# The first layer's q, k and V projections from high and low parts, in token halves, beside the search of the 256 best keys

## The chip, the cores and the metric

The kernel runs on one core of one Trainium2 chip. The metric is the device time of one execution in microseconds (us), the median of several executions. A core has five engines that run their own instruction queues and meet through semaphores: TensorE (PE; its weight loads are listed as PEld), VectorE (DVE), ScalarE (ACT), GpSimd (POOL) and SyncE (SP), which here only issues DMAs.

## The reference

Two transformer layers in sequence on 1024 tokens of width 1024, all in f32. The change lies in the first layer's start:

```
h = x @ w_in                         # [1024, 3112]; parts of its columns:
a_u, a_v      -> gelu, layer norm of v, gMLP mixer (product with w_s)
b_q, b_k, b_v -> diff_attention: 4 heads, two q/k maps of 64 each, V of 128; bias -slope * |distance|
c_q, c_k, c_v -> dsa_attention over 256 selected keys per query
i_q, i_k, i_w -> score = sum over 8 heads of w * relu(q_i . k_i); the 256 best keys of each query are selected
mix = concat(out_a, out_b, out_c);  x = layer_norm(alpha * x + mix @ w_out);  then a gated FFN
```

The second layer has a forgetting attention, a pool mixer, a short convolution, gates and a second FFN; nothing is changed there but the names of some semaphores.

## The kernel before

The program is one hand-written order of work for each engine. `ORDER` lists the stages; a `Ledger` walks through it and gives each weight chunk a slot of the `ring` (4 slots of 128x1024 f32, filled by SyncE's DMAs; a slot is loaded again once its last user has signalled `weights_used`), each chunk that is split into a high and a low part one of three buffers `w_parts` (`w_high`, `w_low`), and each result a pair of PSUM banks.

Two kinds of product are used. A plain f32 product takes `ring` and f32 tiles directly; the trace lists two records for each. A split product works on `float32r` operands: GpSimd (`split_weight`) writes the high part with a TENSOR_SCALAR and the low part, weight minus high part, with a TENSOR_TENSOR, and TensorE sums three products, high with high, high with low, low with high. All later large stages are split; before the change the first layer's input projections are plain.

The order in the stretch that matters, with the stage names of the code:

- `turn_x`, `idx`, `cv`: x is transposed into `xT` (8 tiles of 128 x 1024 tokens), the index and the sparse V projections are made.
- `score`, mixed with `cqk`: 48 score units on TensorE, ScalarE's relu, VectorE's weighted sum.
- VectorE then searches the 256 best keys: 32 bits of a threshold, from the top one down, for six blocks of queries in two groups. For each bit and group: a TENSOR_SCALAR (L2269) and a SCALAR_TENSOR_TENSOR (L2275) on 128x3 numbers set the next trial threshold, then `count` (L2256) compares three blocks of scores with it and counts, one instruction a block. Each waits for the one before it. Then for each block the ties are ranked and the mask is made (`topk_done`), then comes the layer norm of the gMLP's v (`v_normed`).
- TensorE meanwhile runs the rest of `cqk`, `auv` (gMLP's u and v, by tokens), `turn_ws`, `bqk` (q and k of the differential attention: two times four chunks, `by_feature`) and `bv` (its V, `by_token`), all plain f32, from `xT`.
- It then waits for `v_normed`, makes the gMLP product (L1477), waits until VectorE has taken it out of PSUM, and starts the differential attention (`diff.pe`), whose logits VectorE takes with the bias table `bias8`.
- GpSimd makes `dist` at the start, issues the loads of the small constants, and then waits for the masks (`topk_done`). VectorE makes `bias8` from `dist` before its first other work.

What follows (sparse attention, `out1`, FFN, second layer) is not touched.

Of the kernel before, what the change touches and what calls it, by code (L numbers as in the profile page):

```python
# [13 lines left out]
P = 128  # L14
# [49 lines left out]

def sevens(n):
    return [(1, "seven")] * n
# [14 lines left out]
def down_steps(n_k):  # L81
# [11 lines left out]
    "bqk": (whole(4), [0, 1, 2, 3]),  # L93
    "bv": (whole(4), [None, None, None, 3]),
# [28 lines left out]
         ("bqk", 0), ("bqk", 1), ("bv", 0), ("gmlp", 0), ("ada", 0), ("turn_mix", 0), ("out1", 0), ("turn_mod", 0), ("out1", 1)]  # L123
# [21 lines left out]
class Ledger:  # L145


    def __init__(self):
# [6 lines left out]
        for stage, i in ORDER:  # L155
            chunks, units = STAGES[stage] if stage != "idx" else IDX[i]
            self.pairs_at[stage, i] = list(pairs)
            for c, (dmas, kind) in enumerate(chunks):
                s, q = n_loads % RING, n_halves // 2 % PARTS
# [16 lines left out]
                if kind:  # L176
# [5 lines left out]
                    n_halves += 2  # L182
# [51 lines left out]
def program(nc, t, out):  # L234
    L = Ledger()
    with ExitStack() as ctx:
# [32 lines left out]
        xT = view(0, KT, S)  # L269
# [21 lines left out]
        ranks = view(165.5, S)  # L291
# [7 lines left out]
        dist = view(165.5, S)  # L299
# [126 lines left out]
        dist_made = sem("dist_made")  # L426
        bias_made = sem("bias_made")
        lam_sums = sem("lam_sums")
        lam_exps = sem("lam_exps")
# [4 lines left out]
        norm_var = sem("norm_var")  # L434
        norm_sqrt = sem("norm_sqrt")
# [27 lines left out]
        fl_exp, fl_ln, cum_done = sem("fl_exp"), sem("fl_ln"), sem("cum_done")  # L463
        selw_made, counts_made = sem("selw_made"), sem("counts_made")
        cum_high, cum_split, causal_row_made = sem("cum_high"), sem("cum_split"), sem("causal_row_made")
        pool_w_loaded, pool_w_zeroed = sem("pool_w_loaded"), sem("pool_w_zeroed")
# [664 lines left out]
        def b_bias(u, m):  # L1131
            h, b = heads4[u]
            return bias8[:, h, P * (NB - 1 - b):S], bias_made, 4
# [40 lines left out]
        def after_c(act, u):  # L1174
            rows_c(act, u)
            if u == 4:
                act.wait_ge(norm_var, 2)
                act.activation(o_ssq[:, :], o_ssq[:, :], ACT.Sqrt).then_inc(norm_sqrt, 1)
# [117 lines left out]
        def by_feature(pe, stage, i, source):  # L1296

            for c in range(len(STAGES[stage][0])):
                s, p = L.slot(stage, i, c), L.pair(stage, i, c)
                w = ring[:, s, :].rearrange("p (k n) -> p k n", k=KT)  # L1300
                weights_here(pe, stage, i, c)
                pair_here(pe, stage, i, c)
                for h in HALVES:
                    for k in range(KT):
                        mm = pe.matmul(PS[:, 2 * p + h, :], w[:, k, :], source[:, k, half_of(h)],  # L1305
                                       start=(k == 0), stop=(k == KT - 1))
                mm.then_inc(weights_used[s], 1)

        def by_token(pe, stage, source, width=512):

            for c in range(4):
                s = L.slot(stage, 0, c)
                weights_here(pe, stage, 0, c)
                for k in (2 * c, 2 * c + 1):
                    for b in range(NB):
                        p = L.pair(stage, 0, b // 2)
                        if k == 0 and b % 2 == 0:
                            pair_here(pe, stage, 0, b // 2)
                        mm = pe.matmul(PS[:, 2 * p + b % 2, 0:width], source[:, k, tok(b)],  # L1319
                                       ring[:, s, (k % 2) * width:(k % 2 + 1) * width],  # L1320
                                       start=(k == 0), stop=(k == KT - 1))
                        if k == KT - 1 and b % 2 == 1 and b < NB - 1:
                            mm.then_inc(psum_full[p], 1)
                mm.then_inc(weights_used[s], 1)
# [65 lines left out]
        def _(pe):  # L1390
# [68 lines left out]
            by_token(pe, "auv", xT)  # L1459
# [191 lines left out]
        def _(act):  # L1651
# [89 lines left out]
            act.wait_ge(lam_sums, 2)  # L1741
# [25 lines left out]
            for c in range(2):  # L1767
                copy_cqk(1, c)
# [1381 lines left out]
```

## Time and profile before

| | |
|---|---|
| median of 3 runs | 2914.8 us (2908.94 to 2917.13) |
| profiled execution | 2907.3 us, span of its instructions 2905.6 us |
| busy: PE, DVE, ACT, POOL | 2804.6, 1528.2, 932.2, 1278.1 us |
| mean granted TensorE clock | 0.994 |

A busy time is the sum over an engine's instructions. The span is that from the first to the last instruction of the program.

### The profile page before, as it was taken

The numbers are of one execution on the slowest core, as the hardware profiler recorded it, in microseconds if no ns is written. First come the engines' busy times: TensorE is split into PE (matmuls) and PEld (weight loads), VectorE is DVE, ScalarE is ACT, GpSimd is POOL, SyncE is SP. The second block draws the span as 40 slices with busy tenths as digits, with TensorE's granted clock in tenths as the row PEclk, the third lists the DMA queues.
The fourth block names the chain that finished last, engine by engine and source line by source line (L and its number), as shares of the span: only waits on it lengthen the run. The fifth ranks groups of instructions, "written<-read, shape, count | busy, mean of one in ns | idle before, by whom it ended". The sixth has DMA issues, their size and how long they took to land.

```text
span 2905.6 us, 33901 instructions
## 1 busy us (share of the span) xinstructions
PE 2804.6 (97%) x12861; PEld 2071.6 (71%) x12861; DVE 1528.2 (53%) x2414; ACT 932.2 (32%) x1590; POOL 1278.1 (44%) x848
## 2 busy tenths in 40 slices
PE   8999999889999999999999999988999899999998
PEld 5444457468888888887778888855466788888886
DVE  0599977656723334243652203556536722235998
ACT  2401036541233332112333200156103344444443
POOL 2000000036777776666677677700126587753020
PEclk9999999999999999999999999999999999999999
DMA  5111137233422223534433333200556333346854
GB/s 114 30 36 37 40 93 195 88 119 119 131 84 87 87 87 116 211 141 168 129 105 116 123 95 97 71 1 1 180 158 197 117 116 108 117 166 220 280 191 172
DMA packets 343393, 344.59 MB, mean 119 GB/s; under 512 B 18368, under 2 KB 261312, under 8 KB 343232
## 3 DMA queue, kind: packets, MB, share of 16 engines
q1 hardware_dynamic: 319424, 275.33, 30.7%
q10 hardware_dynamic: 21328, 59.97, 5.3%
q0 software_dynamic: 2480, 7.13, 1.0%
q8 instruction: 103, 1.69, 0.2%
q14 instruction: 58, 0.48, 0.0%
HBM read 284.61 MB, written 57.77 MB: 118 GB/s over the span
## 4 chain that ended last, share of the span: by engine, by line
PE 86%; DVE 7%; ACT 2%; issue 2%; DMA 1%; ACTq 0%; POOL 0%; SPq 0%; DVEq 0%; POOLq 0%
PE PS L535 25%; PE PS L1355 13%; PE PS L1367 11%; PE PS L851 9%; PE PS L1319 5%; PE PS L1305 4%; PE PS L1598 4%; PE PS L965 3%; PE PS L1436 2%; PE PS L983 2%; PE PS L1003 2%; PE PS L1547 1%; PE PS L1409 1%; PE PS L995 1%; PE PS L1450 1%
## 5 line engine op out<-in xcount | busy, mean ns | idle before, releaser
L2844 POOL TENSOR_SCALAR w_parts<-ring 128x1024 fp32r<-128x1024 f32 x166 | 205.5, 1238 | 802.3 <-DMA ring<-in_w_out 276.7
L594 DVE TENSOR_TENSOR arena<-arena,PS 128x512 f32<-128x512 f32 x266 | 182.9, 687 | 538.6 <-PE PS L535 537.3
L2847 POOL TENSOR_TENSOR w_parts<-ring,w_parts 128x1024 fp32r<-128x1024 f32 x166 | 445.3, 2682 | 13.8
L851 PE MATMUL PS<-w_parts,hid_high 128*128 128x512 f32 x896 | 276.4, 390 | 5.7 <-DVE w_parts L816 4.1
L535 PE MATMUL PS<-tx_high,w_parts 128*128 128x512 f32 x832 | 264.5, 389 | 0.0
L1355 PE MATMUL PS<-hT_high,w_parts 128*128 128x512 f32 x800 | 248.7, 391 | 7.9 <-DVE hT_low L2439 6.5
L1367 PE MATMUL PS<-w_parts,hid_high 128*128 128x512 f32 x704 | 218.3, 391 | 3.9 <-DVE hid_low L636 2.2
L573 POOL TENSOR_TENSOR w_parts<-arena,w_parts 128x512 fp32r<-128x512 f32 x152 | 194.4, 1291 | 44.6 <-ACT w_parts L554 44.5
L573 POOL TENSOR_TENSOR w_parts<-ring,w_parts 128x512 fp32r<-128x512 f32 x114 | 147.3, 1292 | 131.5 <-ACT w_parts L554 131.5
L851 PEld LDWEIGHTS PS<-w_parts,hid_high 128*128 128x128 f32 x896 | 167.7, 188 | 42.6 <-DVE w_parts L816 6.3
L1355 PEld LDWEIGHTS PS<-hT_high,w_parts 128*128 128x128 f32 x800 | 150.4, 188 | 41.1 <-DVE hT_low L2439 8.2
L535 PEld LDWEIGHTS PS<-tx_high,w_parts 128*128 128x128 f32 x832 | 156.2, 188 | 32.3
L851 PE MATMUL PS<-w_parts,hid_low 128*128 128x512 f32 x448 | 174.3, 389 | 0.0
L1073 DVE CUSTOM_DVE_ANT_0 arena<-PS,arena 128x1024 f32<-128x1024 f32 (+7 forms) x160 | 114.8, 755 | 110.7 <-PE PS L971 53.1
L2256 DVE TENSOR_SCALAR_CACHE_REDUCE arena<-arena,misc 128x384 bf16<-128x384 f32 (+2 forms) x192 | 171.4, 942 | 2.2
L535 PE MATMUL PS<-tx_low,w_parts 128*128 128x512 f32 x416 | 161.8, 389 | 0.0
L1355 PE MATMUL PS<-hT_low,w_parts 128*128 128x512 f32 x400 | 155.8, 389 | 0.0
L1367 PEld LDWEIGHTS PS<-w_parts,hid_high 128*128 128x128 f32 x704 | 132.7, 189 | 32.1 <-issue 4.7
L2907 POOL CAST arena<-ident 128x128 bf16<-128x128 f32 x1 | 0.3, 290 | 335.8 <-DVE arena L2298 335.8
L554 ACT CAST w_parts<-arena 128x512 fp32r<-128x512 f32 x152 | 93.7, 618 | 143.0 <-PE PS L535 120.7
L1319 PE MATMUL PS<-ring,arena 128*128 128x512 f32 (+1 forms) x384 | 138.8, 523 | 0.0
L535 PE MATMUL PS<-x1T_high,w_parts 128*128 128x512 f32 x432 | 138.8, 389 | 0.0
(358 smaller groups left out, 5827.6 us busy)
## 6 DMA issues: line engine op xcount, KB each, us to landing
ring<-in_w_in SPq DMA_DIRECT2D x96, 512.0 KB, 3.7
arena<-hid_spill SPq DMA_DIRECT2D x172, 256.0 KB, 3.7
hid_spill<-arena ACTq DMA_DIRECT2D x54, 512.0 KB, 2.9
ring<-in_w_gu SPq DMA_DIRECT2D x52, 512.0 KB, 3.9
ring<-in_w_ada SPq DMA_DIRECT2D x48, 512.0 KB, 5.3
ring<-in_w_ff SPq DMA_DIRECT2D x96, 256.0 KB, 2.9
ring<-in_w_down SPq DMA_DIRECT2D x44, 512.0 KB, 3.7
ring<-in_w_ff SPq DMA_DIRECT2D x40, 512.0 KB, 4.1
```

Source lines behind the costliest of these rows:

```text
L535: mm = pe.matmul(self.product(g, m), w[:, at], x[:, k, :], start=(k == 0 and i == 0), stop=(k == 3 and i == 2))
L573: pool.tensor_tensor(low, self.raw(n), high.bitcast(F32), ALU.subtract).then_inc(self.split_low, 1)
L594: dve.tensor_tensor(out, a, self.product(g, m), ALU.add).then_inc(self.combined, 1)
L851: mm = pe.matmul(PS[:, 4 * (p % 2) + u, :], x, w, start=(j == 0 and i == 0), stop=(j == self.n_k - 1 and i == 2))
L1305: mm = pe.matmul(PS[:, 2 * p + h, :], w[:, k, :], source[:, k, half_of(h)], start=(k == 0), stop=(k == KT - 1))
L1319: mm = pe.matmul(PS[:, 2 * p + b % 2, 0:width], source[:, k, tok(b)], ring[:, s, (k % 2) * width:(k % 2 + 1) * width], start=(k == 0), sto ...
L1355: mm = pe.matmul(PS[:, 2 * p + bank, :], w[:, q, k * P:(k + 1) * P], x[:, k, half_of(h)], start=(k == order[0] and n == 0), stop=(k == ord ...
L1367: mm = pe.matmul(PS[:, 2 * p + half, :], x[:, k, at], w[:, q, half_of(half)], start=(first and n == 0), stop=(last and n == 2))
L1598: mm = pe.matmul(PS[:, 2 * p + 1, :], w[:, k, :], x[:, half_of(h)], start=(k == ks[0]), stop=(k == ks[-1]))
L2256: stepped(dve.tensor_scalar(tested[b], score[b], threshold(column[b]), None, op, ALU.add, accum_out=enough[:, column[b]:column[b] + 1]))
L2844: pool.tensor_scalar(w_high[:, q, :], ring[:, s, :], 1.0, 1.0, ALU.mult, ALU.mult).then_inc(weights_high, 1)
L2847: pool.tensor_tensor(w_low[:, q, :], ring[:, s, :], w_high[:, q, :].bitcast(F32), ALU.subtract).then_inc(weights_used[s], 1)
```

## The change

- `bqk` and `bv` become split stages. They are done by halves of the tokens: q and k for tokens 0 to 511 (eight chunks), V for them (four chunks), then the same for tokens 512 to 1023. Each weight chunk is so loaded and split twice: 24 loads and splits in place of 12 loads.
- Kind "two" of a chunk: it uses only buffers 1 and 2 of `w_parts` in turn, since buffer 0 shares its memory with live data.
- x itself is needed in a high and a low part. ScalarE copies the high part of a half into free memory (`high_in`), GpSimd subtracts it from `xT` and writes the low part in place (`low_in`), eight tiles of 128x512 for each half. For the second half, the high part overwrites the first half's low part, tile by tile, once the V product of that tile has been made.
- `auv` does its last chunk tile by tile, so that its first tokens' results are complete earlier.
- The bias table moves: `dist` is made by GpSimd after `topk_done`, with the absolute value built from two halves, ScalarE scales it into `bias8`, GpSimd sets the masked corner.
- ScalarE's work is put into one list, `beside_bit`; VectorE's search is as before. Semaphores are merged (`lam_step`, `norm_step`, `fl_step`).

```diff
-    "bqk": (whole(4), [0, 1, 2, 3]),
-    "bv": (whole(4), [None, None, None, 3]),
+    "bqk": (alternate(8), [1, 3, 5, 7]),
+    "bv": (alternate(4), [None, 3]),
...
-         ("bqk", 0), ("bqk", 1), ("bv", 0), ("gmlp", 0), ("ada", 0), ("turn_mix", 0), ("out1", 0), ("turn_mod", 0), ("out1", 1)]
+         ("bqk", 0), ("bv", 0), ("bqk", 1), ("bv", 1), ("gmlp", 0), ("ada", 0), ("turn_mix", 0), ("out1", 0), ("turn_mod", 0), ("out1", 1)]
...
-                s, q = n_loads % RING, n_halves // 2 % PARTS
+                s, q = n_loads % RING, 1 + n_parts % 2 if kind == "two" else n_halves // 2 % PARTS
...
+        def xin(h):
+            return (bqkT_r, xT_r)[h], xT_r
+
+        def in_features(pe, h):
+            x_high, x_low = xin(h)
+            for c in range(8):
+                p, q = L.pair("bqk", h, c // 2), L.part("bqk", h, c)
+                split_here(pe, "bqk", h, c)
+                if c % 2 == 0:
+                    pair_here(pe, "bqk", h, c // 2)
+                for k in range(KT):
+                    if c == 0:
+                        pe.wait_ge(xin_low, KT * h + k + 1)
+                    at = slice(k * P, (k + 1) * P)
+                    pe.matmul(PS[:, 2 * p + c % 2, :], w_high[:, q, at], x_high[:, k, half_of(1 - h)],
+                              start=(k == 0), stop=False)
+                    pe.matmul(PS[:, 2 * p + c % 2, :], w_high[:, q, at], x_low[:, k, half_of(h)], start=False, stop=False)
+                    mm = pe.matmul(PS[:, 2 * p + c % 2, :], w_low[:, q, at], x_high[:, k, half_of(1 - h)],
+                                   start=False, stop=(k == KT - 1))
+                mm.then_inc(parts_used[q], 1)
...
-            by_token(pe, "auv", xT)
+            by_token(pe, "auv", xT, by_tile=True)
...
-            by_feature(pe, "bqk", 0, xT)
-            by_feature(pe, "bqk", 1, xT)
-            by_token(pe, "bv", xT)
+            for h in HALVES:
+                in_features(pe, h)
+                in_tokens(pe, h)
...
+            def high_in(h, k):
+                for b in range(4 * h, 4 * h + 4) if k == 0 else ():
+                    freed(act, "turn_x", b // 4, b % 4)
+                if h == 1 and k % 2 == 0:
+                    q = L.part("bv", 0, k // 2)
+                    act.wait_ge(parts_used[q], L.part_uses("bv", 0, k // 2) + 1)
+                act.copy(xin(h)[0][:, k, half_of(1 - h)], xT[:, k, half_of(h)]).then_inc(xin_high, 1)
...
-            act.wait_ge(bias_made, 4)
+            act.wait_ge(dist_made, 5)
+            for h in range(4):
+                act.activation(bias8[:, h, :], dist, ACT.Copy, scale=-8.0 * SLOPES[h]).then_inc(dist_made, 1)
+            act.wait_ge(dist_made, 5 + 4)
...
-            dve.wait_ge(dist_made, 1)
-            do(dve.scalar_tensor_tensor(out=dist, in0=dist, scalar=-1.0, in1=dist, op0=ALU.mult, op1=ALU.max))
-            for h in range(4):
-                do(dve.tensor_scalar(bias8[:, h, :], dist, -8.0 * SLOPES[h], None, ALU.mult))
-                dve.memset(bias8[0:64, h, S - 64:S], NEG).then_inc(bias_made, 1)
...
+            def low_in(h, k):
+                pool.wait_ge(xin_high, KT * h + k + 1)
+                pool.tensor_tensor(xT_r[:, k, half_of(h)], xT[:, k, half_of(h)],
+                                   xin(h)[0][:, k, half_of(1 - h)].bitcast(F32), ALU.subtract).then_inc(xin_low, 1)
+
+            for c in range(2):
+                split_weight("bqk", 0, c)
+            for k in range(KT):
+                if k % 2 == 0 and k < 6:
+                    s = L.slot("auv", 0, k // 2)
+                    pool.wait_ge(weights_used[s], L.slot_uses("auv", 0, k // 2) + 1)
+                if k == 6:
+                    unit_here(pool, "auv", 0, 1)
+                low_in(0, k)
+            for c in range(2, 8):
+                split_weight("bqk", 0, c)
+            for c in range(3):
+                split_weight("bv", 0, c)
+            low_in(1, 0)
+            low_in(1, 1)
+            split_weight("bv", 0, 3)
+            low_in(1, 2)
+            low_in(1, 3)
+            split_weight("bqk", 1, 0)
+            low_in(1, 4)
+            low_in(1, 5)
+            split_weight("bqk", 1, 1)
+            low_in(1, 6)
+            low_in(1, 7)
+            for c in range(2, 8):
+                split_weight("bqk", 1, c)
+            for c in range(4):
+                split_weight("bv", 1, c)
             pool.wait_ge(topk_done, NB - 2)
+            pool.iota(dist, pattern=[[-1, S]], base=S - P, channel_multiplier=1,
+                      allow_small_or_imprecise_dtypes=True).then_inc(dist_made, 1)
...
```

`in_tokens` makes the V products in the same way: for each chunk two k tiles, four token tiles, three products. SyncE's list of loads follows the new order of stages.

## Rows read from the trace of the kernel before

**Rows 1.** The page's first part: TensorE's busy time, share, instructions.

```profile
PE 2804.6 (97%) x12861; PEld 2071.6 (71%) x12861; DVE 1528.2 (53%) x2414; ACT 932.2 (32%) x1590; POOL 1278.1 (44%) x848
```

**Rows 2.** Chain of waits, 180 to 410 us: start, duration, what.

```profile
181.81 54.93 PE PS L1319 x128
...
237.18 109.87 PE PS L1305 x256
347.05 54.93 PE PS L1319 x128
401.98 3.43 PE PS L1477 x8
```

**Rows 3.** Timeline of VectorE: start, duration, line, operation, idle time before it.

```profile
155.67 0.17 DVE L2269 TENSOR_SCALAR misc<-misc 128x3 int32<-128x3 f32 x1
...
347.80 0.17 DVE L2281 TENSOR_SCALAR misc<-misc 128x6 f32<-128x6 f32 x1
...
391.05 2.29 DVE L2318 TENSOR_TENSOR arena<-arena 128x2048 f32<-128x2048 f32 x1
403.74 1.54 DVE L2325 SCALAR_TENSOR_TENSOR arena<-PS,misc,arena 128x512 f32<-128x512 f32 x2 [10.40 <-PE PS L1477]
```

**Rows 4.** Chain of waits, second layer's V stage.

```profile
1848.29 43.53 PE PS L1547 x192
```

**Rows 5.** The page's DMA issues: count, KB each, us to landing.

```profile
ring<-in_w_in SPq DMA_DIRECT2D x96, 512.0 KB, 3.7
```

**Rows 6.** GpSimd's instructions that write w_parts: ns min/median/max.

```profile
L2844 POOL TENSOR_SCALAR w_parts<-ring x166: 1041/1049/3098, 617.7 to 2339.2; 128x1024 fp32r<-128x1024 f32 x166
L2847 POOL TENSOR_TENSOR w_parts<-ring,w_parts x166: 2352/2394/4376, 618.8 to 2340.3; 128x1024 fp32r<-128x1024 f32 x166
...
L573 POOL TENSOR_TENSOR w_parts<-ring,w_parts x114: 1285/1291/1313, 807.4 to 2568.7; 128x512 fp32r<-128x512 f32 x114
```

**Rows 7.** VectorE's search by groups (busy us, mean ns), one masking instruction.

```profile
L2256 DVE TENSOR_SCALAR_CACHE_REDUCE arena<-arena,misc 128x1024 bf16<-128x1024 f32 x32 | 40.8, 1274 | 0.0
...
L2269 DVE TENSOR_SCALAR misc<-misc 128x3 int32<-128x3 f32 x64 | 10.5, 163 | 0.0
L2275 DVE SCALAR_TENSOR_TENSOR misc<-misc 128x3 int32<-128x3 int32 x62 | 10.1, 163 | 2.1
...
369.67 0.75 DVE L2286 TENSOR_SCALAR arena<-arena,misc 128x1024 bf16<-128x1024 f32 x1
```

**Rows 8.** Timelines of VectorE and GpSimd around 1838 us.

```profile
1838.23 0.91 DVE L2666 TENSOR_TENSOR arena<-arena 64x16 f32<-64x16 f32 x1
1839.17 0.17 DVE L2667 TENSOR_TENSOR arena<-arena 64x16 f32<-64x16 f32 x1
1839.38 3.29 DVE L2668 SCALAR_TENSOR_TENSOR arena<-arena 64x1008 f32<-64x1008 f32 x1
...
1837.60 1.52 POOL L2844 TENSOR_SCALAR w_parts<-ring 128x1024 fp32r<-128x1024 f32 x1 [0.86 <-PE PS L1355]
1839.20 2.40 POOL L2847 TENSOR_TENSOR w_parts<-ring,w_parts 128x1024 fp32r<-128x1024 f32 x1
```

**Rows 9.** The same around 678 us, and one line's durations.

```profile
678.20 1.43 DVE L2378 BATCH_NORM_STATS2 misc<-arena 128x6 f32<-128x512 f32 x2
...
677.60 2.39 POOL L2847 TENSOR_TENSOR w_parts<-ring,w_parts 128x1024 fp32r<-128x1024 f32 x1
...
L2381 DVE TENSOR_SCALAR misc<-misc x4: 170/521/1649, 681.6 to 1418.9; 128x4 f32<-128x4 f32 x4
```

**Rows 10.** TensorE's timeline at 130 us, and a 2 us stretch's sums.

```profile
130.76 3.52 PE L1436 MATMUL PS<-arena,ring 128*128 128x512 f32 x4 [2.99 <-ACT arena L1755]
...
132.00:134.00 2.00, 2.00 (x3) 0.42 (x2) 0.00 (x0) 0.00 (x0) 0.00 (x0) 0.52 0.00 0
```

In the second row the columns are the stretch, its length, the busy us (and instructions) of PE, PEld, DVE, ACT and POOL, the granted TensorE clock, the DMA share and GB/s.

**Rows 11.** Costliest groups of ScalarE: busy us, mean ns.

```profile
L1033 ACT ACTIVATE arena<-arena,misc 128x1024 f32<-128x1024 f32 x20 | 22.9, 1151 | 13.1 <-DVE misc L1073 13.1
```

More of the change, by code:

```diff
@@ L1294, in rows_out, with by_token @@
             act.dma_start(ada_dram[:, 512 * g:512 * (g + 1)], ada_row[0:P:32, g % 2, :]).then_inc(ada_stored, 16)
[L1296 to L1309, printed above, removed]
+        def by_token(pe, stage, source, width=512, by_tile=False):
             for c in range(4):
@@ L1313, in by_token @@
                 weights_here(pe, stage, 0, c)
-                for k in (2 * c, 2 * c + 1):
[L1315 to L1322, printed above, removed]
+                steps = ([(k, b) for b in range(NB) for k in (2 * c, 2 * c + 1)] if by_tile and c == 3 else
+                         [(k, b) for k in (2 * c, 2 * c + 1) for b in range(NB)])
@@ new lines, in by_token @@
+                for k, b in steps:
+                    p = L.pair(stage, 0, b // 2)
+                    if k == 0 and b % 2 == 0:
+                        pair_here(pe, stage, 0, b // 2)
+                    mm = pe.matmul(PS[:, 2 * p + b % 2, 0:width], source[:, k, tok(b)],
+                                   ring[:, s, (k % 2) * width:(k % 2 + 1) * width],
+                                   start=(k == 0), stop=(k == KT - 1))
+                    if k == KT - 1 and b % 2 == 1 and b < NB - 1:
+                        mm.then_inc(psum_full[p], 1)
@@ new lines, in in_tokens @@
+        def in_tokens(pe, h):
+            x_high, x_low = xin(h)
+            for c in range(4):
+                q = L.part("bv", h, c)
+                split_here(pe, "bv", h, c)
+                for k in (2 * c, 2 * c + 1):
+                    at = slice((k % 2) * 512, (k % 2 + 1) * 512)
+                    for n in range(4):
+                        p = L.pair("bv", h, n // 2)
+                        if k == 0 and n % 2 == 0:
+                            pair_here(pe, "bv", h, n // 2)
+                        high, low = x_high[:, k, tok(4 * (1 - h) + n)], x_low[:, k, tok(4 * h + n)]
+                        pe.matmul(PS[:, 2 * p + n % 2, :], high, w_high[:, q, at], start=(k == 0), stop=False)
+                        pe.matmul(PS[:, 2 * p + n % 2, :], high, w_low[:, q, at], start=False, stop=False)
+                        mm = pe.matmul(PS[:, 2 * p + n % 2, :], low, w_high[:, q, at], start=False, stop=(k == KT - 1))
+                        if k == KT - 1 and n == 1:
@@ new lines, in _ @@
+            pool.iota(behind, pattern=[[1, P]], base=0, channel_multiplier=-1,
+                      allow_small_or_imprecise_dtypes=True).then_inc(dist_made, 1)
+            pool.wait_ge(dist_made, 2)
+            for part in (dist[:, S - P:S], behind):
+                pool.tensor_scalar(part, part, 0.0, None, ALU.max).then_inc(dist_made, 1)
+            pool.wait_ge(dist_made, 4)
+            pool.tensor_tensor(dist[:, S - P:S], dist[:, S - P:S], behind, ALU.add).then_inc(dist_made, 1)
+            for h in range(4):
+                pool.wait_ge(dist_made, 5 + h + 1)
+                pool.memset(bias8[0:64, h, S - 64:S], NEG).then_inc(bias_made, 1)
```

129 lines of the change are left out of this document (77 added, 52 removed).

## The prediction

> **What bounds the kernel now.** I read the page first: TensorE is busy for 97% of the span [rows 1], so the reader should expect most of any TensorE saving to arrive, unless another engine stands right behind it. Then the chain of waits through the edited stretch [rows 2]: the gMLP projection (`auv`) runs from 181.81 to 236.74, the q/k products (`bqk`) take 109.87 us, the V products (`bv`) 54.93 us, and at 401.98 the gMLP product (L1477) starts. TensorE never waits in there. Then VectorE's timeline beside it [rows 3]: the search of the 256 best keys runs without a break from 155.67 to 347.80, 64 steps (32 bits, two groups of blocks) of 3.00 us each; ranks, masks and the gMLP normalisation end at 391.05 + 2.29 = 393.34; VectorE then idles 10.40 us until the gMLP product. L1477 waits for both engines. So TensorE sets the time here, but VectorE is only 401.98 - 393.34 = 8.6 us behind. That is the first thing to see: no saving on TensorE can give more than 8.6 us, whatever its size.
>
> **TensorE's part.** Removed: 192 plain f32 products of 128x512, 164.8 us (two records each, 0.858 us a product). Added: 24 chunks (8 q/k and 4 V chunks for each token half) of 24 high/low products, 576 in all. The V stage of the second layer has the same instruction, 192 in 43.53 us, 0.2267 us each [rows 4]: 5.44 us a chunk, 130.6 us in all. The first chunk can start on time. The ring slots come free as `auv` chunks end, the first at 181.81 + 13.73 = 195.5, and a weight load lands in 3.7 us [rows 5], so at 199.2 GpSimd can split; a split is 1.05 us for the high part and 2.39 us for the low part, a low part of x (128x512) 1.29 us [rows 6]. Two splits and eight low parts are 17.2 us, and the last of them waits for the fourth `auv` chunk's first eight products, until about 229, before TensorE is free at 237.18.
>
> In steady state a chunk costs GpSimd 3.52 us with its gap against 5.44 us on TensorE: no stall. At the change of halves, counted from the end of the first V chunk, GpSimd has low parts between the splits: two splits, each followed by two low parts (12.3), the split of the second half's first q/k chunk (15.8), two low parts (18.5), the next split (22.0), two low parts (24.7). TensorE reaches that q/k chunk at 16.3 and should leave it at 21.8, but its last k tile comes at 24.7, and it leaves at 25.4: a stall of 3.6 us. So TensorE ends at 237.18 + 130.6 + 3.6 = 371.4, 30.6 us sooner. That is hidden: it is 22 us ahead of VectorE's 393.34.
>
> **VectorE's part.** Its own work in the stretch is unchanged. Taken off it is the bias table, which lay in idle time at the start and gives nothing. What is new is GpSimd's company: it did nothing during the search, and now has 24 splits and 16 low parts, 24 x 3.44 + 16 x 1.29 = 103.2 us of work, between 199.2 and the last split. That one starts when the chunk two before the last is off TensorE, 371.4 - 10.9 = 360.5, and ends at 364. All of this lies beside the search.
>
> A search step is a TENSOR_SCALAR and a SCALAR_TENSOR_TENSOR on 128x3 (163 ns each), then three counts at about 1.2 ns an element (128x1024: 1274 ns) [rows 7]. What do such operations do beside GpSimd? A 64x16 TENSOR_TENSOR with two SBUF inputs that starts at 1838.23 takes 0.91 us and ends 0.02 us after GpSimd's instruction (1837.60 + 1.52); the next, before GpSimd's next one, takes 0.17; the one at 1839.38 takes 3.29 us because GpSimd holds on until 1841.60 [rows 8]. A 128x4 TENSOR_SCALAR takes 170 ns or 1649 ns. The large single-input BATCH_NORM_STATS2 runs its usual 0.7 us each in the middle of GpSimd's 2.39 us [rows 9]. So the two small operations of each step should wait for GpSimd's current instruction to end, and the counts should not. A TENSOR_SCALAR that writes bf16 without a count takes 0.75 us on 128x1024, the count 1.27 us [rows 7]: the count does not run at the double rate, which is why I put it with the unaffected ones.
>
> The Trainium skill ("GPSIMD Engine Reference", Key points) says that GpSimd shares its SBUF interfaces with VectorE and contends with instructions in a two-port mode or with two SBUF inputs; the trace agrees (0.91 and 3.29 us above), and by that rule the search is no longer undisturbed once GpSimd works beside it.
>
> The price. A step that arrives at random in the 165 us from 199.2 to 364 waits on average (24 x (1.05²/2 + 2.39²/2) + 16 x 1.29²/2) / 165 = 95.1 / 165 = 0.58 us for the first small operation. GpSimd may also start an instruction in the 0.19 us between the two small ones: 0.19 x 103.2 / 165, about 0.12 us, less the cases where the first has just waited. Together 0.69 us. A step then takes 3.69 us, 44.7 of them fit into the 165 us, and they lose 30.9 us. Low end: only the second operation waits, 165 / 3.58 x 0.58 = 26.6 us, and as the two engines are both periodic the phase may take some 6 us off that, 20. High end of this kind: after each wait the other small operation is caught too, and one search step passes per chunk: 24 x (5.44 - 3.00) = 58.6 us. I take 30.9, since in [rows 8] the operation right behind a waiting one slips through in 0.17 us. Highest: the counts wait too, at most all of GpSimd's work, 103 us.
>
> The Trainium skill ("VectorE: DVE Perf Modes", Mode 2×_2P) lets a one-tensor operation use both ports where its outermost dimension is even, or odd and equal on both sides; 128x3 to 128x3 would then be caught. No row here has a 3-wide operation beside GpSimd; without the rule the lost time would be the 26.6 us above and the result +19.9 us.
>
> **The join.** The gMLP product starts when VectorE is through: 393.34 + 0.1 + 30.9 = 424.3. TensorE has then idled from 371.4, 53 us. After a wait of only 2.99 us at 130.76 its granted clock stood at 0.52 (the 1.2 GHz level), and four records took 3.52 us where L1477 needs 1.72 for four [rows 2, 10]: 1.8 us more. From there on everything is as before. ScalarE and GpSimd also build the bias table after the search. GpSimd's few small operations start when the masks are done, 17 us before the join; ScalarE has the square root 9.7 us after the masks, two copies, then four copies of 128x1024 at about 1.15 us [rows 11]: ready about when the normalisation ends, and first needed some 16 us later. Nothing, and with that cover gone 4.6 us.
>
> Sum: -8.6 + 0.1 + 1.8 + 30.9 = **+24.2 us**. The profiled execution took 2907.3 us for its span of 2905.6, 7.5 us under the median of the three shown; the difference put on the median gives 2914.8 + 24.2 = **2939 us**.
>
> **Rivals.**
> 1. *No collision* (not slower). The 3-wide operations pass beside GpSimd, or hold the interface too briefly to wait. For it: no row shows that width; against: every two-input operation of 16 or 8 elements that meets GpSimd's instruction waits. It gives -8.6 + 0.1 + 1.8 = -6.7 us, 2908, inside what can be told from no change. The sign turns measurable at a lost search time of 6.7 + 8.7 = 15.4 us, 0.31 us a step.
> 2. *Both small operations are caught*: 58.6 - 6.7 = up to +52 us, 2967. For it: the gap between high and low split is only 0.08 us, so a race of 0.02 us decides; against: the pair at 1838.23 and 1839.17.
> 3. *The counts are caught too*: up to 103.2 - 6.7 = +96 us, 3011. Against: BATCH_NORM_STATS2. For: the counts read a threshold from SBUF as well.
> 4. *TensorE becomes the bound* because GpSimd starves it: it would have to lose 53 us on top of 3.6, more than half of GpSimd's whole work. Under 1 in 50.
> 5. *A gain that can be measured*: over 0.3% faster needs 8.7 us, and VectorE leaves 8.6 less the cold clock; only scatter gets there.
>
> **Numbers.** 0.3% (8.7 us) is about what a measurement of this kernel can tell from no change. My forecast 0.60, with its own range 2928 to 2946 (lost time 20 to 38 us). Rival 2 0.15, rival 3 0.06, no collision 0.12, a weaker collision near the turning point 0.04, rivals 4 and 5 together 0.03. Range 2925 to 2971: it takes in the forecast and rival 2, and leaves out rival 3 and most of the no-collision case. Slower 0.83 (forecast, 2, 3 and half of the weaker collision), same 0.13, faster 0.04.
>
> **What the profile after would show.** Right: L2269 and L2275 with a mean well above 163 ns, together about 30 us more busy time over their 126 instructions, the counts still 1274 ns, the search ending near 379 and L1477 starting near 424, TensorE idle for about 50 us before it with a granted clock near 0.5 at the restart; w_parts products from 237 to about 371. Wrong: small operations at 163 ns with L1477 near 393 (rival 1), longer counts (rival 3), or L1477 released by TensorE's own work (rival 4). The prediction fails if the race behind a waiting operation goes the other way, or if the 3-wide operations are exempt.

## The result and the profile after

The changed kernel takes 2947.85 us (median of four, 2947.45 to 2950.32) against 2912.83 us (median of four) for the kernel before on the same chip: ratio 1.0122, 95% interval 1.0104 to 1.0139, slower. Forecast were 2939 us and slower. The range 2925 to 2971 holds the result; the narrower range of the main forecast, 2928 to 2946, does not. The profiled execution took 2947.9 us for a span of 2946.2, 40.6 above the span of before; the difference of the medians is 35.0, since the profiled run of before was a short one. The terms below are compared within the spans.

The page of the changed kernel, its first part and the row of the granted clock:

```profile
span 2946.2 us, 34405 instructions
PE 2779.2 (94%) x13046; PEld 2112.4 (72%) x13053; DVE 1568.7 (53%) x2405; ACT 945.2 (32%) x1610; POOL 1391.0 (47%) x920
...
PEclk9999959999999999999999999999999999999999
```

Beside [rows 1]: TensorE has 25 us less work and the kernel is longer, so the engine that fell (97% to 94% of the span) is not what sets the time. VectorE's work rose by 40.5 us though its list of work did not grow (it even lost the bias table): something it does has become slower. The row of the granted clock (PEclk, in tenths of full speed for 40 equal slices) shows a 5 at one place, where TensorE idled. The groups of VectorE's instructions between 150 and 440 us, by shape, say what became slower (instructions | busy us, mean ns | idle before):

```profile
L2333 DVE TENSOR_SCALAR misc<-misc 128x3 int32<-128x3 f32 x64 | 44.5, 695 | 0.0
L2320 DVE TENSOR_SCALAR_CACHE_REDUCE arena<-arena,misc 128x1024 bf16<-128x1024 f32 x32 | 40.8, 1275 | 0.0
...
L2339 DVE SCALAR_TENSOR_TENSOR misc<-misc 128x3 int32<-128x3 int32 x62 | 19.4, 312 | 2.1
```

These answer [rows 7]; L2269, L2275 and L2256 are now L2333, L2339 and L2320. 64 and 62 instructions that took 163 ns each, 10.5 + 10.1 us in all, take 44.5 + 19.4 us, 43.3 us more. The count is where it was, 1275 ns against 1274. A waiting operation shows as a long one here, not as idle time before it (0.0): idle columns would have missed all of it.

VectorE's timeline at the end of the search and at the end of the normalisation, of the changed kernel:

```profile
389.79 1.14 DVE L2320 TENSOR_SCALAR_CACHE_REDUCE arena<-arena,misc 128x896 bf16<-128x896 f32 x1
...
390.97 0.17 DVE L2345 TENSOR_SCALAR misc<-misc 128x6 f32<-128x6 f32 x1
...
434.35 2.29 DVE L2382 TENSOR_TENSOR arena<-arena 128x2048 f32<-128x2048 f32 x1
```

The search ends at 390.97, in [rows 3] at 347.80. The rest of VectorE's stretch, the ranks, masks and normalisation (the rank part, below), has its old length, 45.7 us against 45.5, and it ends at 434.35 + 2.29 = 436.64. The chain of waits there, and the granted clock in windows of 2 us (us, then each engine's busy time, the clock, DMA share, GB/s):

```profile
431.11 5.64 issue
436.75 6.05 PE PS L1509 x8
```

```profile
436.00:438.00 2.00, 1.25 (x2) 0.77 (x3) 0.64 (x1) 0.62 (x1) 0.79 (x1) 0.50 0.00 0
438.00:440.00 2.00, 2.00 (x3) 0.74 (x3) 0.00 (x0) 0.00 (x0) 0.00 (x0) 0.50 0.00 0
440.00:442.00 2.00, 2.00 (x4) 0.86 (x3) 1.43 (x2) 0.00 (x0) 0.00 (x0) 0.62 0.00 0
442.00:444.00 2.00, 0.79 (x2) 0.00 (x0) 1.20 (x3) 0.00 (x0) 0.00 (x0) 1.00 0.00 0
```

TensorE's V products end at 373.43. It idles for 63 us until the gMLP product (L1509, L1477 before), which runs at 0.50, the 1.2 GHz level, for its first 3 us and more, and takes 6.05 us for what took 3.43 in [rows 2]. The first logits of the differential attention on ScalarE, in the changed kernel and in the kernel before:

```profile
447.96 1.15 ACT L1037 ACTIVATE arena<-arena,misc 128x1024 f32<-128x1024 f32 x1 [11.34 <-DVE misc L1077]
```

```profile
410.58 1.15 ACT L1033 ACTIVATE arena<-arena,misc 128x1024 f32<-128x1024 f32 x1 [5.95 <-DVE misc L1073]
```

They start 37.4 us later, which is -8.6 (slack) + 0.1 (handover) + 43.3 + 2.6 (cold clock). The other 3.2 us between the spans are scattered over small waits after that point; I did not trace them to a cause.

How a wait comes about: some of VectorE's small operations (the counts between them are left out) and GpSimd's instructions in one stretch of the changed kernel.

```profile
249.28 0.17 DVE L2333 TENSOR_SCALAR misc<-misc 128x3 int32<-128x3 f32 x1
249.47 2.23 DVE L2339 SCALAR_TENSOR_TENSOR misc<-misc 128x3 int32<-128x3 int32 x1
...
254.15 0.51 DVE L2333 TENSOR_SCALAR misc<-misc 128x3 int32<-128x3 f32 x1
254.69 0.16 DVE L2339 SCALAR_TENSOR_TENSOR misc<-misc 128x3 int32<-128x3 int32 x1
...
260.49 2.08 DVE L2333 TENSOR_SCALAR misc<-misc 128x3 int32<-128x3 f32 x1
...
248.13 1.05 POOL L2909 TENSOR_SCALAR w_parts<-ring 128x1024 fp32r<-128x1024 f32 x1 [1.92 <-PE PS L1335]
249.27 2.42 POOL L2912 TENSOR_TENSOR w_parts<-ring,w_parts 128x1024 fp32r<-128x1024 f32 x1
253.57 1.06 POOL L2909 TENSOR_SCALAR w_parts<-ring 128x1024 fp32r<-128x1024 f32 x1 [1.88 <-PE PS L1335]
254.71 2.42 POOL L2912 TENSOR_TENSOR w_parts<-ring,w_parts 128x1024 fp32r<-128x1024 f32 x1
259.01 1.05 POOL L2909 TENSOR_SCALAR w_parts<-ring 128x1024 fp32r<-128x1024 f32 x1 [1.88 <-PE PS L1335]
260.15 2.40 POOL L2912 TENSOR_TENSOR w_parts<-ring,w_parts 128x1024 fp32r<-128x1024 f32 x1
```

Three cases in eleven microseconds. At 254.15 the TENSOR_SCALAR meets the high split (253.57 + 1.06 = 254.63) and ends at 254.66; the next operation slips into the 0.08 us before the low split. At 260.49 it meets the low split and waits until 262.57, 0.02 us after its end. At 249.28, within 0.01 us of the start of a low split, it just gets through, and the SCALAR_TENSOR_TENSOR behind it waits until that split ends (249.47 + 2.23 = 251.70 against 249.27 + 2.42 = 251.69). The Trainium skill ("SBUF — State Buffer", Who interferes with whom) says that VectorE and GpSimd share a pair of ports under a lock held for a whole instruction, and that a VectorE instruction with one SBUF input outside a two-port mode is free of it; the trace agrees with both, by the ends of the waits and by the counts' 1275 ns.

### The profile page after: what moved, and what is told of

Read it like the earlier page. It is cut to its first block, busy times and chain, and to the rows that moved or that the text cites. A ratio compares the mean times of both kernels' runs of the same rounds, so it can differ in the third digit from the quotient of the medians.

```text
span 2946.2 us, 34405 instructions
## 1 busy us (share of the span) xinstructions
PE 2779.2 (94%) x13046; PEld 2112.4 (72%) x13053; DVE 1568.7 (53%) x2405; ACT 945.2 (32%) x1610; POOL 1391.0 (47%) x920
## 4 chain that ended last, share of the span: by engine, by line
PE 77%; DVE 17%; issue 3%; ACT 2%; DMA 1%; ACTq 0%; POOL 0%; DVEq 0%; SPq 0%; POOLq 0%
PE PS L539 24%; PE PS L1387 13%; PE PS L1399 11%; PE PS L855 9%; DVE arena L2320 6%; PE PS L1630 4%; PE PS L969 3%; PE PS L987 2%; PE PS L1007 2%; PE PS L1579 1%; PE PS L1441 1%; DVE misc L2333 1%; PE PS L999 1%; PE PS L1482 1%; PE PS L1311 1%
## 5 line engine op out<-in xcount | busy, mean ns | idle before, releaser
L2909 POOL TENSOR_SCALAR w_parts<-ring 128x1024 fp32r<-128x1024 f32 x190 | 236.4, 1244 | 996.7 <-DMA ring<-in_w_out 281.3
L2912 POOL TENSOR_TENSOR w_parts<-ring,w_parts 128x1024 fp32r<-128x1024 f32 x190 | 501.0, 2637 | 15.8
L855 PE MATMUL PS<-w_parts,hid_low 128*128 128x512 f32 x448 | 174.3, 389 | 0.0
L2320 DVE TENSOR_SCALAR_CACHE_REDUCE arena<-arena,misc 128x384 bf16<-128x384 f32 (+2 forms) x192 | 171.5, 943 | 2.3
L1399 PE MATMUL PS<-w_parts,hid_low 128*128 128x512 f32 x352 | 137.6, 391 | 0.0
L969 PE MATMUL PS<-arena 64*128 64x512 f32 (+2 forms) x480 | 119.1, 525 | 18.4 <-DVE misc L1077 15.5
```

The costliest lines, as they stand in the source:

```text
L855: mm = pe.matmul(PS[:, 4 * (p % 2) + u, :], x, w, start=(j == 0 and i == 0), stop=(j == self.n_k - 1 and i == 2))
L969: mm = pe.matmul(PS[:, 2 * m + c // 512, 0:w], self.q(j, m, b), self.k(j, m, c, w), start=True, stop=more[m] is None)
L1399: mm = pe.matmul(PS[:, 2 * p + half, :], x[:, k, at], w[:, q, half_of(half)], start=(first and n == 0), stop=(last and n == 2))
L2320: stepped(dve.tensor_scalar(tested[b], score[b], threshold(column[b]), None, op, ALU.add, accum_out=enough[:, column[b]:column[b] + 1]))
L2909: pool.tensor_scalar(w_high[:, q, :], ring[:, s, :], 1.0, 1.0, ALU.mult, ALU.mult).then_inc(weights_high, 1)
L2912: pool.tensor_tensor(w_low[:, q, :], ring[:, s, :], w_high[:, q, :].bitcast(F32), ALU.subtract).then_inc(weights_used[s], 1)
```

## The experiments

Times are medians with their ratio to the kernel before on the same chip (2911.2 to 2911.9 us), where more than one run was made. "Lost" is the busy time of the search's two small operations above their undisturbed time: 10.5 + 10.1 us with two groups [rows 7], 5.5 + 5.1 us with one group (as in e6). Of each edit the main lines are shown.

**e1: GpSimd's work left out.** The high and low parts of this stretch are not made (zeros stand in for both parts of the weights, x's high part for its low part), so q, k and V are not the reference's; everything else of the change stays.

```
+                if stage in ("bqk", "bv"):
+                    pool.sem_inc(weights_high, 1)
+                    pool.sem_inc(weights_used[s], 1)
+                    return
```

> The changed kernel with GpSimd's 24 splits and 16 low parts left out: TensorE runs the same 576 products on the same schedule, but on parts that nobody computed (zeros for the weights, the high part in place of x's low part), so q, k and V are not the reference's. Theory (VectorE's two small operations of each search step wait for GpSimd's instructions): L2333 and L2339 are back at 163 ns, the search takes 192.1 us again, VectorE is through at about 393, and the time is that of before - 8.6 + 0.1 + 2.6 (cold restart of TensorE) = -5.9 us, about 2907. Rival (the loss comes from the doubled weight loads, the cold clock or the new order on ScalarE): still 2935 or more, with the search no shorter than in the changed kernel.

2903.14 us, ratio 0.9969 (0.9958 to 0.9981). The two groups of VectorE's small operations in this kernel:

```profile
L2333 DVE TENSOR_SCALAR misc<-misc 128x3 int32<-128x3 f32 x64 | 10.5, 164 | 0.0
L2339 DVE SCALAR_TENSOR_TENSOR misc<-misc 128x3 int32<-128x3 int32 x62 | 10.1, 162 | 2.1
```

The search ends at 348.66, L1509 starts at 394.44. GpSimd's company costs the whole loss: 44.7 us lie between this kernel and the changed one. Without it the change gains 8.1 us (5.5 to 12.2 by the interval). VectorE's slack less the cold clock is -8.6 + 0.1 + 2.1 = -6.4 us, and the first logits start 5.4 us sooner than in the kernel before; TensorE is done 25.8 us before L1509, and that gains nothing.

**e2: GpSimd's instructions in quarters.** The changed kernel, each split in 128x256 pieces, each low part of x in two.

```
+                for r in at:
+                    ins = pool.tensor_scalar(w_high[:, q, r], ring[:, s, r], 1.0, 1.0, ALU.mult, ALU.mult)
```

> The changed kernel, but each of GpSimd's 128x1024 instructions of the split as four of 128x256, each low part of x as two of 128x256: the same result. Theory (a small operation waits for the end of the one instruction that GpSimd is in): a wait is at most about 0.66 us, the search loses 15 to 22 us in place of 43, time 2922 to 2929. Rival (the loss goes with GpSimd's total busy time, whatever the length of an instruction): 43 us lost as before, about 2948 or a little more.

2925.15 us, 1.0052 (1.0035 to 1.0069), as expected. The same work of GpSimd in smaller instructions loses 17.4 us in place of 43.3.

**e3 and e4: dummy work of GpSimd beside the kernel before.** Subtractions on free memory beside its search, each waiting for the one before: 40 of 128x1024, or 160 of 128x256.

```
+            for r in range(40):
+                do(pool.tensor_tensor(scratch[:, 2, 0:1024], scratch[:, 0, 0:1024], scratch[:, 1, 0:1024], ALU.subtract))
```

> The kernel before, with forty TENSOR_TENSORs of 128x1024 added on GpSimd from the start of the search, on free memory, each waiting for the one before; the products stay plain f32. Theory with lock-step (a released step starts right after an instruction's end, so it meets the second next one's end): a step takes two GpSimd periods of about 2.5 us, 5.0 us in place of 3.0; 20 steps in 100 us, 40 us lost, +34 us after the 8.6 us of slack and 2.6 us of cold clock, about 2947. Random arrival, as in the prediction's sum: 1.2 us a step, 28 us lost, about 2935. No collision: 2913.

> The same with 160 instructions of 128x256, each about 0.66 us with 0.15 us between: the same amount of elements. Theory: a wait is at most 0.66 us; some 15 us lost, +9 us, about 2922. Rival (the loss goes with GpSimd's total busy time): as much as with the forty long ones. No collision: 2913.

2940.55 and 2912.08 us, one run each. The groups of e3, then of e4:

```profile
L2270 DVE TENSOR_SCALAR misc<-misc 128x3 int32<-128x3 f32 x64 | 47.5, 741 | 0.0
L2276 DVE SCALAR_TENSOR_TENSOR misc<-misc 128x3 int32<-128x3 int32 x62 | 10.0, 162 | 2.1
L2911 POOL TENSOR_TENSOR arena<-arena 128x1024 f32<-128x1024 f32 x40 | 94.3, 2358 | 3.1
```

```profile
L2270 DVE TENSOR_SCALAR misc<-misc 128x3 int32<-128x3 f32 x64 | 19.4, 304 | 0.0
L2276 DVE SCALAR_TENSOR_TENSOR misc<-misc 128x3 int32<-128x3 int32 x62 | 10.1, 162 | 2.1
L2911 POOL TENSOR_TENSOR arena<-arena 128x256 f32<-128x256 f32 x160 | 116.6, 729 | 12.5
```

94.3 us of long instructions lose 36.9 us, 116.6 us of short ones 9.0: it is the length of an instruction that VectorE pays for, not GpSimd's busy time. Both sizes were missed: e3's time lies between the two expectations (2947 in lock-step, 2935 for random arrival), so that only the trace decides between them, and e4 lost 9.0 us where 15 were expected. With a semaphore's gap between GpSimd's instructions the second small operation never waits. And the waits are not random ones. Three in a row of the first small operation in e3, where a random arrival would wait 1.2 us on average (an estimate, half of an instruction's 2.36 us):

```profile
232.98 1.84 DVE L2270 TENSOR_SCALAR misc<-misc 128x3 int32<-128x3 f32 x1
...
237.46 2.25 DVE L2270 TENSOR_SCALAR misc<-misc 128x3 int32<-128x3 f32 x1
...
242.75 1.84 DVE L2270 TENSOR_SCALAR misc<-misc 128x3 int32<-128x3 f32 x1
```

A wait puts VectorE at the end of a GpSimd instruction, from where its next steps come at fixed distances. From 232.98 to 242.75 two steps take 9.77 us, which is four instructions of GpSimd's 2.43 us spacing. From 164.77 to 247.22 all eighteen waits alternate between 1.83 to 1.84 and 2.23 to 2.25 us: the two engines lock in phase.

**e5 and e6: one group of blocks.** The search's six blocks in one group, so 32 steps of 128x6, in the changed kernel (e5) and in the kernel before (e6).

```
-            groups = ((2, 3, 7), (4, 5, 6))
+            groups = ((2, 3, 4, 5, 6, 7),)
```

> The changed kernel with the search's six blocks in one group: a bit has one pair of small operations on 128x6 in place of two on 128x3, the same counts, the same result. Theory (the loss is a wait for each pair that meets GpSimd): undisturbed the search would take 32 x 5.7 = 182 us, 10 less; some 26 pairs meet GpSimd at 0.7 to 1.1 us each, 18 to 28 us lost, net +8 to +18 against the search of before, time 2913 to 2923. Rival (loss proportional to GpSimd's work, not to the number of pairs): 43 - 10, about 2938.

> The kernel before with the same one group. Theory: TensorE sets the time there, VectorE only gets 10 us more slack: no difference, 2911 within 3 us. Rival (VectorE's search is already on the path before): up to 10 us less.

e5: 2916.06 us, 1.0016 (1.0006 to 1.0025). e6: 2912.72 us, 1.001 (1.0001 to 1.0019). Half the steps bring 7.1 us of lost time, not half of 43.3 (means of 282 and 281 ns for the two operations): a 5.73 us step runs beside a 5.44 us chunk and mostly comes at a free moment: 8 of its 63 small operations wait. But the search then ends sooner, at 348.10, and GpSimd's last splits fall beside the rank part, whose large operations wait for GpSimd too (a 384-wide TENSOR_TENSOR_SCAN takes 3.03 us, in e6 0.96): from the search's end to the normalisation's it takes 56.0 us, in e6 45.5. e6 itself shows that VectorE does not set the end before the change: its search ends 6.8 us sooner, and it idles 19.07 us before L1477's result, no gain.

**e7: high parts on ScalarE.** In the changed kernel; GpSimd keeps one 2.40 us instruction for each chunk, and x's low parts, 78 us of work in place of 103.

```
+                act.copy(w_high[:, q, :], ring[:, s, :]).then_inc(weights_high, 1)
```

> The changed kernel with the high parts of the 24 chunks copied by ScalarE; GpSimd keeps one TENSOR_TENSOR of 2.36 us a chunk and x's low parts: the same result. GpSimd's work beside the search falls from 103 to 78 us. Theory, random arrival: 24 x 2.36 squared / 2 and the x parts give 0.49 us a step, with the gap catches 0.58, 46 steps, 27 us lost, 2932; in lock-step up to one step a chunk, 2.4 us each, as bad as before the move, 2948. Rival (TensorE needs the splits sooner than ScalarE's queue gives them): a TensorE idle time in the product stage of more than 50 us.

2948.89 us, 1.0132 (1.0116 to 1.0147). 25 us less work of GpSimd, and the loss is about the same, 42.1 us (means of 659 and 331 ns), as the lock-step branch of the expectation had it. By the prediction's formula, a random arrival would have given back some 4 us. The long instruction alone keeps up a fixed pattern: of four steps two wait, at 329.45 and 334.72 for 2.24 and 2.40 us, and the same again at 345.77 and 351.04.

**e8: e2, e5 and e7 together.** ScalarE's high parts, GpSimd's low parts in quarters, one group.

> High parts on ScalarE, GpSimd's low parts in instructions of 128x256, one group in the search: the same result. Theory: a wait is at most 0.7 us, some 26 pairs at 0.2 to 0.35 us, 5 to 9 us lost against 10 us won by the one group, so VectorE is through at about 390, and the time is 2911 - 8.6 + 2.6 - 1 to - 5, 2899 to 2904: faster than both kernels. If the waits add up differently, up to 2912.

2917.4 us, 1.0019 (1.001 to 1.0029): a miss by 13 us of the 2899 to 2904 expected, and 5 us above the 2912 allowed for. The search ends at 357.69. One instruction has 11.1 of the 16.8 us lost. VectorE's small operations around it, and GpSimd's run beside it, from its timeline:

```profile
293.46 0.80 DVE L2355 TENSOR_SCALAR misc<-misc 128x6 int32<-128x6 f32 x1
...
300.31 11.32 DVE L2355 TENSOR_SCALAR misc<-misc 128x6 int32<-128x6 f32 x1
```

```profile
297.68 2.83 POOL L3000 TENSOR_TENSOR xT_r<-xT,xT_r 128x256 fp32r<-128x256 f32 x4
300.48 2.82 POOL L2938 TENSOR_TENSOR w_parts<-ring,w_parts 128x256 fp32r<-128x256 f32 x4
303.25 2.83 POOL L3000 TENSOR_TENSOR xT_r<-xT,xT_r 128x256 fp32r<-128x256 f32 x4
306.05 2.81 POOL L2938 TENSOR_TENSOR w_parts<-ring,w_parts 128x256 fp32r<-128x256 f32 x4
308.82 2.78 POOL L3000 TENSOR_TENSOR xT_r<-xT,xT_r 128x256 fp32r<-128x256 f32 x4
```

It ends at 311.63, 0.03 us after the last of this unbroken run of small instructions. That made a theory: an unbroken run shuts VectorE out as one long instruction would. The first row above already speaks against it: the same run, 32 instructions without a gap, began at 289.31, and the operation at 293.46 got in after 0.80 us.

**e9: unbroken runs beside the kernel before.** e4 with only every eighth subtraction waiting; the eight of a run write eight different places of the free memory, where e4's all wrote one.

```
+                if r % 8 == 7:
+                    do(ins)
```

> The kernel before with the 160 small subtractions of e4 (128x256 on free memory) again, but only every eighth waits for the one before it: 20 unbroken runs of eight, each run about 5.6 us long, with a gap between runs. Computation of the outputs is unchanged. Theory A (an unbroken run of GpSimd instructions shuts VectorE's small operation out as one long instruction would, seen once in e8 at 300.31 for 11.32 us): the longest TENSOR_SCALAR 128x3 is over 3 us, and the search loses about 5.6 us in every other step while the runs last, 40 us or more in all, though no instruction is longer than 0.75 us; 2940 us or more. Theory B (the 11.32 us was something else, and a waiting operation gets in after the instruction that it met): no TENSOR_SCALAR over 0.9 us, a loss near e4's 11 us, 2908 to 2918 us.

2928.13 us, one run.

```profile
L2276 DVE SCALAR_TENSOR_TENSOR misc<-misc 128x3 int32<-128x3 int32 x62 | 21.6, 349 | 2.1
L2270 DVE TENSOR_SCALAR misc<-misc 128x3 int32<-128x3 f32 x64 | 20.8, 325 | 0.0
L2912 POOL TENSOR_TENSOR arena<-arena 128x256 f32<-128x256 f32 x160 | 110.6, 728 | 1.6
```

The theory falls: none of the 64 TENSOR_SCALARs takes over 0.72 us, so a waiting operation gets in after the instruction that it met. e2 says the same: beside its unbroken runs of twelve, which write `w_parts` and x's low part in turn, no small operation takes over 0.71 us. The time lies between the two expectations (2908 to 2918, and 2940 or more). Without the gaps the second small operation is now caught as well (0.64 us in 24 of its 62 cases): 21.9 us lost against e4's 9.0. In the changed kernel the same is seen where GpSimd's low parts of x stand back to back with the splits: at 299.89 and 301.83 the pair takes 1.91 and 1.22 us, at 305.49 and 307.80 it takes 2.28 and 1.18.

**e10 and e11: gaps.** e10 is e8 with each piece of GpSimd waiting for the one before; e11 is e2 and e5 together, with such gaps, the high parts back on GpSimd.

```
+                    if n_pieces > 1:
+                        do(ins)
```

> e8 again (ScalarE makes the high parts, GpSimd the low parts in pieces of 128x256, the search's six blocks in one group), with each of GpSimd's pieces now waiting for the one before it. If the unbroken run was what e8 lost its time to: no TENSOR_SCALAR 128x6 over 0.9 us, the search ends about 11 us sooner (346 to 348), the normalisation's end comes at 393 to 396, and the time is 2900 to 2907 us, below before's. If small pieces are no cure and VectorE loses as much over many of them: the search ends at 355 or later and the time stays at 2914 to 2920 us.

> e2 and e5 together with gaps: the changed kernel with GpSimd's splits and low parts of this stretch in pieces of 128x256, each piece waiting for the one before it, and the search's six blocks in one group. More pieces than in e10 (208 against 128), so more chances to meet one. By e2's mean of 0.27 us a step over 32 steps: some 8 us lost in the search (end near 348), a few us more in the rank part, 2903 to 2911 us. If the gaps between GpSimd's pieces delay its low parts so that TensorE waits for them, TensorE's products end later than 375 and the time rises above 2915 us.

e10: 2911.85 us, 0.9999 (0.9989 to 1.0008). The search behaves as expected, no small operation over 0.76 us, its end at 346.35; but the rank part beside the last five splits takes 53.9 us, the normalisation ends at 400.2 rather than 393 to 396, and the time misses the 2900 to 2907 expected. e11: 2921.07 us, 1.0031 (1.0019 to 1.0043), which is the second branch of its expectation: TensorE's products end late, at 413.7, and the time is above 2915. The search is hardly disturbed and ends at 344.66; by then TensorE is some 13 us behind e5, but most of its delay comes afterwards, because now GpSimd waits for VectorE. From its chain of waits:

```profile
391.50 2.56 POOL w_parts L2921
394.13 2.66 POOL w_parts L2921
396.86 2.66 POOL w_parts L2921
399.59 0.73 POOL w_parts L2921
400.41 0.79 PE PS L1351
...
413.70 1.72 PE PS L1509 x4
```

The rank part's and the normalisation's large operations stand nearly back to back on VectorE, and GpSimd's 0.73 us pieces now take 2.6 (one from 394.13 to 396.79 lies over a normalisation step that ends at 396.20). The splits become the chain, TensorE is starved, and L1509 waits for its own engine until 413.70. That the gaps let VectorE in ahead of each piece is argued and not shown: e8's pieces without gaps have a mean of 1.00 us beside the rank part, e11's 1.36 and e10's 1.06, but no run has e11's order without its gaps.

**e12: GpSimd's work placed beside the counts.** e10, with each low part during the search waiting for the two small operations of a set step, and then one instruction again (128x1024) beside the counts; only the last five splits stay in quarters.

```
+            def after_step(i):
+                pool.wait_ge(topk_step, 14 + 8 * i)
...
+            plan = {8: [0], 10: [1, "a0", "a1"], 11: ["a2", "a3"], 12: ["a4", "a5"], 13: ["a6", "a7"],
+                    15: [2], 16: [3], 17: [4], 18: [5], 19: [6], 20: [7], 21: [8], 22: [9],
+                    23: [10, "b0", "b1"], 24: [11, "b2", "b3"], 25: [12, "b4", "b5"], 26: ["b6", "b7", 13],
+                    27: [14], 28: [15], 29: [16], 30: [17], 31: [18]}
```

The numbers are chunks, "a" and "b" the low parts of x's first and second half.

> GpSimd's work is put where VectorE doesn't need to get in. As e10 (ScalarE makes the high parts, the search's six blocks in one group), but each of GpSimd's low parts during the search waits until VectorE has done the two small operations of a set step of the search, and is then one instruction again (128x1024, 2.40 us) beside the 5.3 us of counts that follow; only the last five splits, which fall beside VectorE's rank part, stay in pieces of 128x256. If the only loss is that of small operations that meet a GpSimd instruction: TENSOR_SCALAR 128x6 and SCALAR_TENSOR_TENSOR 128x6 have means under 0.18 us, the search ends at 341 (in e6, undisturbed, 340.97) though GpSimd works beside it for as long as in e7, the rank part loses 5 to 8 us, the normalisation ends at 392 to 395, and the time is 2901 to 2906 us, below before's by some 8. If long GpSimd instructions slow the counts too, the counts' mean rises over 0.95 us and the search ends later than 345. If TensorE is starved by the waits (its products end later than 385), the time stays at 2910 us or above.

2904.95 us (11 runs), 0.998 (0.9971 to 0.9989), faster than both kernels. Its groups of small operations and of GpSimd's long ones, and VectorE's last operation of the normalisation:

```profile
L2355 DVE TENSOR_SCALAR misc<-misc 128x6 int32<-128x6 f32 x32 | 5.7, 177 | 1.1
L2361 DVE SCALAR_TENSOR_TENSOR misc<-misc 128x6 int32<-128x6 int32 x31 | 5.1, 166 | 1.1
L2938 POOL TENSOR_TENSOR w_parts<-ring,w_parts 128x1024 fp32r<-128x1024 f32 x19 | 45.6, 2399 | 222.9 <-DVE misc L2361 180.3 <-ACT w_parts L1834 35.7 <-DVE arena L2342 6.9
```

```profile
390.27 2.29 DVE L2404 TENSOR_TENSOR arena<-arena 128x2048 f32<-128x2048 f32 x1
```

19 instructions of the very kind that e7 has, beside the counts, cost 0.2 us (small operations of 5.7 + 5.1 us, in e6 5.5 + 5.1). The search takes 188.5 us from its start at 150.66, in the undisturbed e6 188.3. e7's 42 us are not all the work of the placement, since one group of blocks alone brought the loss to 7.1 us in e5; the nearest run, e10, has the same but for the placement and the pieces, and there the search takes 194.0 us and the whole 2911.85. The remaining loss is the rank part's, 53.4 us for 45.5. L1509 starts at 392.67, 9.3 us before [rows 2], and pays 2.5 us for the cold clock.

## Why the prediction was right, and where its size was off

- **Who sets the time before.** "VectorE is only 8.6 us behind": held. With the collision taken away (e1) the change gives 8.1 us, and a shorter search alone (e6) gives none.
- **TensorE's part.** Predicted end 371.4, measured 373.43. At the change of halves TensorE waits 2.6 us for the low parts (predicted 3.6); the products behind that wait run at a granted clock of 0.50 from 310 to 314, a term that the prediction lacked, and the two together cost 5.8 us (from the first to the last of these products 136.6 us, in e1 130.8). As said, it is hidden.
- **Which operations wait.** Both small ones, one input or two, and never the counts: right, in the changed kernel and in e3. This was taken from rows with other shapes at 1838 us [rows 8], the nearest that the trace had.
- **The price of the collision** is the term that was mis-sized: 30.9 predicted, 43.3 measured, inside its bounds of 20 and 58.6, but outside the 20 to 38 that the main forecast gave itself. That 2947.85 still lies in the stated range it owes to the room left for rival 2, most of which did not come true: of the number, that much is luck. The step that failed is "a step that arrives at random". A step that has waited starts at the end of a GpSimd instruction, and both engines are periodic. In the steady stretches three chunks (16.3 us) hold four steps, and their waits repeat: at 325.81, 330.85, 334.21 and 337.01 the TENSOR_SCALAR takes 2.40, 0.33, 0.17 and 2.08 us, and at 342.13, 347.17, 350.53 and 353.33 the same within 0.01. That is 1.1 us a step where 0.69 was assumed. e3 and e7 show it apart from the rest: beside equal instructions the waits repeat in a fixed pattern, and a quarter less of GpSimd's work (e7) loses as much. The prediction noted the phase, but as something that could only take time off.
- **The second small operation.** "Slips through" was right for a wait that ends at the gap between high and low split, wrong where GpSimd has no gap, at the change of halves (290 to 309 us), where both wait; e9 shows that by itself. Altogether it has 9.3 us of the 43.3, where the prediction had 0.11 us a step, 4.9 us.
- **The join.** 424.3 predicted, 436.75 measured: the 12.4 us of the collision. The cold clock costs 2.6 in place of 1.8; the product has eight records, and the estimate came from four.
- **The bias table**: nothing, as said. ScalarE's four copies start at 430.99 and the first logits that need it come at 447.
- **Rivals.** No collision, and caught counts, are both refuted by the groups after. Of rival 2 a part is true (pairs that both wait), not the whole. Rival 4, a starved TensorE, did not occur in the changed kernel, but e11 brings it about, mostly because GpSimd waits for VectorE's large operations and not by GpSimd's amount of work.

In sum: -8.6 + 0.1 + 2.6 + 43.3 = +37.4 at the join against +24.2, and 3.2 us of scatter behind it.

## What to carry to other kernels

Before work goes to an idle GpSimd, look at what VectorE does beside it: a chain of small dependent operations pays for the length of GpSimd's instructions, not for their share of the time, and two periodic engines should be counted step by step in phase, not by an average wait. Long GpSimd instructions are free beside VectorE operations that don't take part in the collision (here the counts), so place them there with a semaphore, as e12 does. Cutting them short helps less (17.4 us are still lost in e2), and in e11, cut short and with gaps, it was GpSimd that waited.

## What the runs showed of the hardware

- A small VectorE operation that waits ends 0.01 to 0.03 us after a GpSimd instruction, in all runs, and with one exception (e8, below) it is the instruction that it met; 128x3 and 128x6 TENSOR_SCALARs with one input wait as two-input ones do.
- VectorE's large operations and GpSimd's stretch each other: the 384-wide TENSOR_TENSOR_SCAN took 3.03 us in e5 and 0.96 in e6; in e12 the quarter splits beside the rank part have a mean of 1214 ns, in e4 729.
- The 11.32 us wait in e8 passed over some sixteen GpSimd instructions. Unbroken runs of eight (e9) and of twelve that write two tiles in turn (e2) do not show it, an earlier wait in the same run of 32 lasted 0.80 us, and it is absent with gaps (e10). Its cause stays open.
- The cold clock's price at the gMLP product does not grow with the time that TensorE had idled: 2.6 us after 63 us, 1.7 after 66 (e7), 3.1 after 30 (e5), 2.1 after 26 (e1), 2.5 after 18 (e12), 3.1 after 18 (e10).
